# Experts' up projections in steps of 512 inner columns: half-contraction tiles of 512 columns, products of 512, wider evictions and transposes

## The reference, cut to what matters

```python
def swiglu(x, w1, w3, w2):
    return (jax.nn.silu(x @ w1) * (x @ w3)) @ w2
...
    def expert_block(args):
        tok_b, e_b = args
        xb = x2[tok_b]
        return swiglu(xb, w1[e_b], w3[e_b], w2[e_b])
```

## Time and profile before

| what | value |
|---|---|
| median of 3 runs | 3476.21 us (3470.22 to 3481.88) |
| the profiled execution, its own time | 3476.61 us |
| span of its core, first to last instruction | 3474.8 us |
| mean granted TensorE clock over the span | 0.971 |
| PE busy / DVE busy / ACT busy | 3299.8 / 2332.3 / 1838.8 us |
| HBM read | 718.64 MB |

### The profile page before, as it was taken

How to read it: one execution, slowest core, us unless ns; L and a number is a source line. 1 busy time by engine, 2 the same in 40 slices (tenths; PEclk the granted TensorE clock), 3 DMA queues, 4 the chain that set the end, 5 groups by cost and what they waited for, 6 DMA issues and landing times.

```text
span 3474.8 us, 56477 instructions
## 1 busy us (share of the span) xinstructions
PE 3299.8 (95%) x24379; PEld 3047.0 (88%) x24379; DVE 2332.3 (67%) x2986; ACT 1838.8 (53%) x2194; POOL 0.2 (0%) x4
## 2 busy tenths in 40 slices
PE   8999999999899899999999999899799999999798
PEld 7988999999889799999999999888587889985698
DVE  6876655578766588888888888745565556465454
ACT  5464544454635377777777777633443444335343
POOL 0000000000000000000000000000000000000000
PEclk9999999999999899999999999999799999999899
DMA  6432565454325599899899899611233456530353
GB/s 249 170 134 97 182 231 194 158 194 146 134 97 184 214 373 351 327 355 350 333 351 352 334 352 344 252 68 61 109 111 134 141 222 233 211 127 13 134 191 112
DMA packets 102815, 723.43 MB, mean 208 GB/s; under 512 B 11680, under 2 KB 13344, under 8 KB 16672
## 3 DMA queue, kind: packets, MB, share of 16 engines
q1 hardware_dynamic: 102560, 719.73, 56.3%
HBM read 718.64 MB, written 1.05 MB: 207 GB/s over the span
## 4 chain that ended last, share of the span: by engine, by line
PE 77%; DVE 12%; ACT 8%; issue 2%; DMA 1%; SPq 0%; DVEq 0%; ACTq 0%
PE PS L1534 13%; PE PS L1535 13%; PE PS L1536 13%; PE PS L1487 6%; PE PS L1485 6%; PE PS L1486 6%; DVE WL L2244 4%; ACT WH L1855 3%; PE PS L1793 3%; PE PS L1791 3%; PE PS L1792 3%; PE PS L1632 2%; PE PS L1601 2%; PE PS L1564 1%; PE PS L1577 1%
## 5 line engine op out<-in xcount | busy, mean ns | idle before, releaser
L2244 DVE TENSOR_TENSOR WL<-RAW,WH 128x2048 fp32r<-128x2048 f32 (+2 forms) x428 | 963.0, 2252 | 578.0 <-ACT WH L1855 572.4
L1855 ACT ACTIVATE WH<-RAW 128x2048 fp32r<-128x2048 f32 (+2 forms) x428 | 802.6, 1878 | 252.7 <-PE PS L1536 183.6
L1534 PE MATMUL PS<-PH,WH 128*128 128x256 f32 x2464 | 710.8, 288 | 39.2 <-DVE PL L2440 7.9
L1536 PE MATMUL PS<-PH,WL 128*128 128x256 f32 x2464 | 697.2, 283 | 0.0
L1535 PE MATMUL PS<-PL,WH 128*128 128x256 f32 x2464 | 697.2, 283 | 0.0
L2244 DVE TENSOR_TENSOR WL<-F,WH 128x2048 fp32r<-128x2048 f32 x210 | 481.2, 2292 | 87.4 <-ACT WH L1855 86.4
L1534 PE MATMUL PS<-HPH,WH 128*128 128x256 f32 (+1 forms) x1648 | 496.7, 301 | 24.6 <-DVE HPL L2330 12.6
L1534 PEld LDWEIGHTS PS<-PH,WH 128*128 128x128 f32 x2464 | 471.2, 191 | 47.9 <-issue 29.2
L1535 PE MATMUL PS<-HPL,WH 128*128 128x256 f32 (+1 forms) x1648 | 481.2, 292 | 0.0
L1536 PE MATMUL PS<-HPH,WL 128*128 128x256 f32 (+1 forms) x1648 | 480.8, 292 | 0.0
L1535 PEld LDWEIGHTS PS<-PL,WH 128*128 128x128 f32 x2464 | 471.1, 191 | 1.3
(11 more groups left out here) (382 smaller groups left out, 5072.8 us busy)
## 6 DMA issues: line engine op xcount, KB each, us to landing
F<-in_moe_w SPq DMA_DIRECT2D x210, 1024.0 KB, 5.5
RAW<-in_ffn_w SPq DMA_DIRECT2D x130, 1024.0 KB, 4.9
RAW<-in_moe_w SPq DMA_DIRECT2D x126, 1024.0 KB, 5.1
RAW<-in_w_in SPq DMA_DIRECT2D x64, 1024.0 KB, 4.9
F<-in_ada_w SPq DMA_DIRECT2D x18, 1024.0 KB, 11.5
RAW<-in_w_kv SPq DMA_DIRECT2D x16, 1024.0 KB, 4.9
G<-in_ada_w SPq DMA_DIRECT2D x15, 1024.0 KB, 10.4
RAW<-in_w_in_ab SPq DMA_DIRECT2D x12, 1024.0 KB, 5.0
```

Of the source, the lines that this page charges most:

```text
L1534: T_.matmul(out, lh, rh, start=first, stop=False)
L1536: last = T_.matmul(out, ll, rh, start=False, stop=end)
L1855: S.activation(mem["WH"][:, t.s % NHL, 0:m], v.raws[t.slot][:, 0:m], ACT.Copy).then_inc(*ac.done("w_hi", t.s))
L2244: V.tensor_tensor(mem["WL"][:, t.s % NHL, 0:m], v.raws[t.slot][:, 0:m], mem["WH"][:, t.s % NHL, 0:m].bitcast(F32), sub).then_inc(*dv.done( ...
```

## The change

The up tiles are cut the other way: 512 rows of 512 columns in place of 1024 rows of 256. The bytes and the number of tiles stay (1 MB, 28 up tiles and 14 down tiles per expert), and the host lays `moe_w1` and `moe_w3` out for it. A step now covers 512 inner columns, so there are 7 per expert:

- `up(e, j, which, half)` handles one tile: 4 row blocks x 3 = 12 matmuls of 512 columns, into a whole bank; `half` 0 starts the sum and `half` 1 ends it.
- The silu eviction, the gate multiplication, and the two copies after the transposes are 512 columns wide and half as many; `turn` does four transposes.
- The order within a step is up `w1` half 0, turn (step before), up `w1` half 1, up `w3` half 0, down, up `w3` half 1, down. `finish`, `sel`, `gather` and `context_sums` hang on the same positions (`beside`), at twice the pace per step; in the last expert two sums and the norm's middle go behind the last `turn`.
- The silu on ACT now waits for the second `w1` tile in the unit of that tile. `TMP1` is used as two rows of 512 in place of four of 256, and the ring of turned rows holds two double steps.

```diff
-    def up(e, j, which):
-        t = p.weight(("up", part, e, j, which), io["moe_w1" if which == 0 else "moe_w3"][e], j)
-        t.end = ("up", part, e, j, which)
+    def up(e, j, which, half):
+        t = p.weight(("up", part, e, j, which, half), io["moe_w1" if which == 0 else "moe_w3"][e], 7 * half + j, 4, 512)
+        t.end = ("up", part, e, j, which, half)
         out.append(("tile", t.key))
-        p.bank(t.end, MOEB)
-        if which == 1:
-            p.tmp.take(("tmp", "moe", part, e, j), TMP4)
-        put("up", e, j, which)
+        if half == 0:
+            p.bank(("up", part, e, j, which), MOEB)
+        elif which == 0:
+            p.tmp.take(("tmp", "moe", part, e, j), (0, 2))
+        put("up", e, j, which, half)
...
+    def beside(e, j, at):
+        if j == 1 and at == 0 and e:
+            finish(e - 1)
+        if e % 2 and e < 7:
+            if j == 3 and at == 0:
+                put("sel", e + 1)
+            elif j > 3 and 2 * j - 8 + at < 5:
+                gather(e + 1, 2 * j - 8 + at)
+        if e == 7 and part == 0 and 2 * j + at > 6:
+            context_sums(2 * j - 7 + at)
     for e in range(8):
-        for j in range(14):
-            pe_, pj = (e, j - 1) if j else (e - 1, 13)
-            up(e, j, 0)
+        for j in range(7):
+            pe_, pj = (e, j - 1) if j else (e - 1, 6)
+            up(e, j, 0, 0)
             if pe_ >= 0:
                 turn(pe_, pj)
-            up(e, j, 1)
+            up(e, j, 0, 1)
+            up(e, j, 1, 0)
+            if pe_ >= 0 and (e, j) != (7, 6):
+                down(pe_, 2 * pj)
+            beside(e, j, 0)
+            up(e, j, 1, 1)
+            if (e, j) == (7, 6):
+                down(pe_, 2 * pj)
             if pe_ >= 0:
-                down(pe_, pj)
-                if pj == 13:
+                down(pe_, 2 * pj + 1)
+                if pj == 6:
                     put("leave", pe_)
...
+            beside(e, j, 1)
+    turn(7, 6)
+    if part == 0:
+        for k in (7, 8, 9):
+            context_sums(k)
+    down(7, 12)
     down(7, 13)
...
-        out = bank(key)[:, 0:256]
-        product(out, [(v.xg(e, 0, k), v.xg(e, 1, k), w.h[:, k, :], w.l[:, k, :]) for k in range(8)]).then_inc(*pe.done("ps", *key))
+        if half == 0:
+            pe.freed(plan.banks.before[key])
+        out = PS[:, plan.banks.place[key], :]
+        for k in range(4):
+            xh, xl = v.xg(e, 0, 4 * half + k), v.xg(e, 1, 4 * half + k)
+            T_.matmul(out, xh, w.h[:, k, :], start=half == 0 and k == 0, stop=False)
+            T_.matmul(out, xh, w.l[:, k, :], start=False, stop=False)
+            last = T_.matmul(out, xl, w.h[:, k, :], start=False, stop=half == 1 and k == 3)
+        last.then_inc(*pe.done("ps", *key, half))
...
-        for k in range(2):
+        for k in range(4):
             last = T_.transpose(out[:, k * 128:k * 128 + 128], tm[:, k * 128:k * 128 + 128], ident)
...
-        if which:
+        if which == 0 and half == 1:
             key = ("tmp", "moe", part, e_, j)
-            ac.wait_ge("ps", "up", part, e_, j, 0)
+            ac.wait_ge("ps", "up", part, e_, j, 0, 1)
...
-        if which:
-            key = ("tmp", "moe", part, e_, j)
-            y = mem["TMP1"][:, plan.tmp.place[key], :]
+        if which and half:
+            y = v.hid(plan.tmp.place["tmp", "moe", part, e_, j])
```

More of the change, by code:

```diff
@@ L708, in splits_ahead @@
         elif kind == "up":
-            at["up", args[3], args[0], args[1], args[2]] = pos
+            at["up", args[4], args[0], args[1], args[2], args[3]] = pos
         elif kind == "down":
@@ L884, in first_order @@
             p.apply("f1")
-            p.put("tile", ("up", 0, 0, 0, 0), 1)
+            p.put("tile", ("up", 0, 0, 0, 0, 0), 1)
             p.bank(("router",), (7,))
@@ L1390, in views, with hs @@
     v.gate_col = lambda e: mem["GC"][:, e % 3:e % 3 + 1]
-    v.hs = lambda e, j: (p2.h[:, (14 * e + j) % 4, :], p2.l[:, (14 * e + j) % 4, :])
+    def hs(e, j, n=1):
+        i = (14 * e + j) % 4
+        return tuple(x[:, i:i + n, :].rearrange("p a n -> p (a n)") for x in (p2.h, p2.l))
+    v.hs = hs
+    v.hid = lambda i: mem["TMP1"][:, i:i + 2, :].rearrange("p a n -> p (a n)")
     return v
@@ L1763, in gather, with up @@
             last.then_inc(*pe.done("ps", "g", part, e, i))
-    def up(e, j, which, part):
+    def up(e, j, which, half, part):
         key = ("up", part, e, j, which)
-        w = weight(key)
-        for i in range(8):
+        w = weight(key + (half,))
+        for i in (0, 1, 4, 5) if half == 0 else (2, 3, 6, 7):
             pe.wait_ge("free_a", "g", part, e - e % 2, i)
-        out = bank(key)[:, 0:256]
-        product(out, [(v.xg(e, 0, k), v.xg(e, 1, k), w.h[:, k, :], w.l[:, k, :]) for k in range(8)]).then_inc(*pe.done("ps", *key))
+        if half == 0:
[7 more added lines that the diff above has]
+        last.then_inc(*pe.done("ps", *key, half))
     def turn(e, j, part):
-        out, tm = bank(("tr", part, e, j)), mem["TMP1"][:, plan.tmp.place["tmp", "moe", part, e, j], :]
+        out, tm = bank(("tr", part, e, j)), v.hid(plan.tmp.place["tmp", "moe", part, e, j])
         pe.wait_ge("free_d", "up", part, e, j, 1)
-        for k in range(2):
+        for k in range(4):
             last = T_.transpose(out[:, k * 128:k * 128 + 128], tm[:, k * 128:k * 128 + 128], ident)
@@ L1782, in down @@
         w, (oh, ol) = weight(("dn", part, e, j)), v.hs(e, j)
-        pe.wait_ge("free_d", "tr", part, e, j)
+        pe.wait_ge("free_d", "tr", part, e, j // 2)
         if j == 0 and e:
@@ L2114, in gather @@
                 if x >= 3:
-                    ac.wait_ge("ps", "up", part, x - 3, 13, 1)
+                    ac.wait_ge("ps", "up", part, x - 3, 6, 1, 1)
                 dst = v.xg(x, i // 4, 2 * (i % 4), 2).rearrange("p (k c) -> p k c", k=2)
@@ L2118, in gather, with up @@
             last.then_inc(*ac.done("free_a", "g", part, e_, i))
-    def up(e_, j, which, part):
-        if which:
+    def up(e_, j, which, half, part):
+        if which == 0 and half == 1:
             key = ("tmp", "moe", part, e_, j)
-            ac.wait_ge("ps", "up", part, e_, j, 0)
+            ac.wait_ge("ps", "up", part, e_, j, 0, 1)
             ac.freed(plan.tmp.before[key])
-            S.activation(mem["TMP1"][:, plan.tmp.place[key], :], bank(("up", part, e_, j, 0))[:, 0:256], ACT.Silu).then_inc(
+            S.activation(v.hid(plan.tmp.place[key]), bank(("up", part, e_, j, 0)), ACT.Silu).then_inc(
                 *ac.done("free_a", "up", part, e_, j, 0))
@@ L2129, in turn @@
         ac.wait_ge("ps", "tr", part, e_, j)
-        n = 14 * e_ + j
+        n = 14 * e_ + 2 * j
         if n >= 4:
-            ac.wait_ge("ps", "dn", part, (n - 4) // 14, (n - 4) % 14)
-        S.activation(v.hs(e_, j)[0], bank(("tr", part, e_, j))[:, 0:256], ACT.Copy).then_inc(*ac.done("hs_hi", part, e_, j))
+            ac.wait_ge("ps", "dn", part, (n - 3) // 14, (n - 3) % 14)
+        S.activation(v.hs(e_, 2 * j, 2)[0], bank(("tr", part, e_, j)), ACT.Copy).then_inc(*ac.done("hs_hi", part, e_, j))
     def leave(e_, part):
@@ L2694, in gather, with up @@
             V.tensor_copy(v.gate_col(x), bank(("g", part, x, "gc"))[:, 0:1]).then_inc(*dv.done("free_d", "g", part, x, "gc"))
-    def up(e_, j, which, part):
-        if which:
-            key = ("tmp", "moe", part, e_, j)
-            y = mem["TMP1"][:, plan.tmp.place[key], :]
+    def up(e_, j, which, half, part):
+        if which and half:
+            y = v.hid(plan.tmp.place["tmp", "moe", part, e_, j])
             dv.wait_ge("free_d", "g", part, e_, "gc")
             dv.wait_ge("free_a", "up", part, e_, j, 0)
-            dv.wait_ge("ps", "up", part, e_, j, 1)
-            V.scalar_tensor_tensor(y, y, v.gate_col(e_), bank(("up", part, e_, j, 1))[:, 0:256], mult, mult).then_inc(
+            dv.wait_ge("ps", "up", part, e_, j, 1, 1)
+            V.scalar_tensor_tensor(y, y, v.gate_col(e_), bank(("up", part, e_, j, 1)), mult, mult).then_inc(
                 *dv.done("free_d", "up", part, e_, j, 1))
     def turn(e_, j, part):
-        oh, ol = v.hs(e_, j)
+        oh, ol = v.hs(e_, 2 * j, 2)
         dv.wait_ge("hs_hi", part, e_, j)
-        V.tensor_tensor(ol, bank(("tr", part, e_, j))[:, 0:256], oh.bitcast(F32), sub).then_inc(*dv.done("free_d", "tr", part, e_, j))
+        V.tensor_tensor(ol, bank(("tr", part, e_, j)), oh.bitcast(F32), sub).then_inc(*dv.done("free_d", "tr", part, e_, j))
     def leave(e_, part):
@@ L3003, in lay_out @@
         "w_in_ab": packed(x["w_in_ab_2"][0]), "w_out_ab": packed(x["w_out_ab_2"][0]), "w_out_c": packed(x["w_out_c_2"][0], 2, 1024),
-        "moe_w1": np.stack([packed(w) for w in x["moe_w1"][0]]), "moe_w3": np.stack([packed(w) for w in x["moe_w3"][0]]),
+        "moe_w1": np.stack([packed(w, 4, 512) for w in x["moe_w1"][0]]), "moe_w3": np.stack([packed(w, 4, 512) for w in x["moe_w3"][0]]),
         "moe_w2": np.stack([packed(w, 2, 1024) for w in x["moe_w2"][0]]),
```

10 lines of the change are left out of this document (removed).

## The result

| | kernel before | changed kernel |
|---|---|---|
| median, range (5 runs each) | 3471.42 us (3470.16 to 3481.88) | 3451.3 us (3447.54 to 3459.14) |
| ratio, 95% interval | 1 | 0.9936 [0.9916, 0.9956] |
| profiled execution, its span | 3476.61 us, 3474.8 us | 3447.54 us, 3445.8 us |

The change makes the kernel faster by 20 us. Of the 7.7 us between 3459.0 and 3451.3, 3476.2 - 3471.4 = 4.8 come from the level that the sum started from, a median of three runs, and 20.1 - 17.2 = 2.9 from the size of the gain.

A forecast was written before the change was run, and what follows sets the result against it. PE was taken to bound the experts' stretch; 16.7 us from up products plus 0.7 at the end came off 3476.61 us, other terms 0, giving 3459.0 against the median. Range 3451 to 3471, main case 3454 to 3465 (81%).

The forecast's parts named there:

- the spare times: Slack before PE wants a low half in plain double steps: 0.66 us behind the silu, 0.68 us behind the turn.
- The bound, and the up products: Experts' stretch goes at PE's pace; 12 products of 512 columns replace 24 of 256, saving 0.075 us per tile, 16.7 us.
- the `down` row: Profile row of the same step's down tile: 12 products of 512 columns in 2.80 us, taken as the new up price.
- the two rivals that priced the product at 0.240 or half way: Up products: no fixed cost saved, 3475.5 us, chance 8%; or only half the gain, 3467.1 us, chance 7%.
- the forecast's estimate of 0.03 us per tile: Up products by the skill's rule, N/2.4 + 2.5 ns: 2.62 against 2.59 us per tile, 6.7 us in all; not adopted.
- The slower rival: Second `w3` tile's low half comes late every double step once its path is 0.66 us longer; 3494 us, chance 4%.
- Copies, banks, transposes, loads: Wider evictions, bank reuse, four transposes per double step and weight loads: each taken as 0; transposes might save 4.5 us.
- The two ends: Last expert's end: one PE wait instead of two (0.98 + 1.02 us), gain 0.7 us, between -0.6 and 2; start gains nothing.
- The clock: One half-clock dip of about 3.4 us in a gather step, costing 1.7 us, may go, stay or double: 0 +- 2.
- A clock below 1.00 in the stretch: Listed among the signs that would show the forecast wrong: PE's clock falling within the experts' stretch.
- The sum: 16.7 us from up products plus 0.7 from the end: 17.4 us off the profiled 3476.61, giving 3459.0 against the median.
- The low end of the range, 3451: Wide range's lower edge, reached if cheaper transposes (up to 4.5 us) and one clock dip less come together.

## Why the forecast was wrong, and which of its steps held

The pace of the stretch, its bound and the spare times came out as forecast. What was wrong is the step from the stretch to the total, and inside the stretch several terms are off that cancel.

*The bound, and the up products: right, a little small.* The stretch goes at PE's pace, and an up tile took the pace of the `down` row, 2.80 us. The kernel with narrow products shows that this, and no other part, carries the gain. The forecast took 0.075 us a tile from starts given to 0.01 us, between 0.07 and 0.08. The seven double steps say 0.080 each, 17.8 us for 223 tiles in place of 16.7; and by the same rows the two rivals that priced the product at 0.240 or half way fall: they would have given double steps of 17.6 and 17.4. So does the forecast's estimate of 0.03 us per tile, worked out from the rule that the Trainium skill gives for an isolated product (page "TensorE: Matmul & The Clock Gate", section "Back-to-back issue gap"); this trace, with 0.080, does not agree with it.

*The slower rival: false, and its threshold right.* No split came late. The kernels with extra silus put the point from which it decides between 0.52 and 0.92 us of added path; the forecast said 0.66. Past that point a double step with a late split lost 0.43 us.

*Copies, banks, transposes, loads: right.* 599, 741, 683 and 600 ns against estimates of 580, 740, 680 and 600. Four transposes cost what two pairs did. Loads never held anything up: a window of plain double steps (1510 to 1544.5 us) moved 363 GB/s, where the forecast had reckoned with 365, with PE busy throughout. No wait of PE stands at a gather or a `leave` of a plain step. A double step with a `finish` is 19.57 us before and 19.14 after, so it lost 0.11 us more than a plain one; seven of them are 0.8 us that the forecast had no term for.

*The two ends: gain about twice as large.* At the end PE idles 0.56 us where the kernel before idled 0.98 + 1.02: 1.4 us in place of 0.7, since the norm sums stand inside the wait. At the start the two waits of 1.02 us of the kernel before (the second is the `WL` wait of the earlier trace rows) became one of 2.16.

*The clock: past its bound.* Three dips of about 3.4 us at half the clock (1.2 GHz) lie in the changed kernel's stretch, near 1210, 1660 and 1914 us, where before had one. "A clock below 1.00 in the stretch" was one of the forecast's own signs of being wrong, and it came. A double step of the second gather with a dip is 22.15 us, the one of the first gather without one 20.61 (turn to turn), so a dip costs 1.5 us here, and in the kernel before 21.38 - 19.99 = 1.4; the difference of the two kernels is 3 x 1.5 - 1.4 = 3.1 us, where the forecast allowed 2. Ahead of the second and the third PE was busy without a pause, at a granted clock of 1.00 (1640 to 1659 us, 1895 to 1912 us). What stands just ahead of both is the first step of a gather, some 2.2 us of products of 8 rows and of one column, as it does ahead of the dip of the earlier trace rows:

```profile
1657.27 0.60 PE L1774 MATMUL PS<-SM,PH 128*128 128x1 f32 x4
...
1659.68 0.57 PE L1796 MATMUL PS<-WH,PH 128*128 128x512 f32 x1
```

Not every such step is followed by a dip: in the nine profiles in which it is not cut in two, 13 of 27 are.

*The sum.* In the stretch 17.8 + 1.4 + 0.8 - 3.1 = 16.9 us by these terms, 17.2 measured. The kernel with narrow products fits them: without the 17.8 it should keep 1.4 + 0.8, less 1.6 for one dip more than before, 0.6 us, and it kept 1.1. So the 17.4 of the forecast came out near the measured 17.2 by luck: up products, ends and `finish` gave 2.6 us more than the sum had, and the dips took 3.1 back.

*What failed* is the step from the stretch to the total. The sum was set against one execution "0.4 us above the median shown", as if three runs fixed the level at 3476.2; the kernel before measured 3471.4, 3472.1, 3475.0 and 3475.3 later on. And the sum has no term for what lies behind the stretch: it puts that at nothing without a reason, while the same 8272 matmuls took 1228.3 to 1242.3 us there in ten profiles. The changed kernel measured 21 us less in all and 17 in the stretch: 4 us that no term has. The low end of the range, 3451, was to be reached by transposes that cost less and a dip that goes; four transposes cost 0.46 us, as two pairs did, and two dips came on top. That 3451.3 lies beside that end is luck.

*What stays open.* Whether these 4 us are real. 17.2 us would be a ratio of 0.9950, which lies inside each of the three intervals. On the other hand, in all eight measurements of wide tiles (narrow products among them) the median fell by more than the stretch did, by 0.6 to 8.6 us, and in that of the old tiles in another order by 0.6 less; several of them share their runs of the kernel before, so they are fewer than eight witnesses.

Behind the stretch the two profiles of old tiles show 1242.3 and 1240.8 us, the eight of wide tiles 1228.3 to 1239.1, with a mean of 1234.8. That hints at some microseconds gained there, though no instruction there was changed, and with two profiles of one kind it proves nothing. The granted clock of that part is 0.95 or 0.96 in every profile, and PE's busy time moves along with its length (1144.1 in the shortest, 1156.7 in one of the longest), so the half-clock spells in it are the likeliest carrier. An estimate from windows of 1 us, PE's busy time in each times what the granted clock lacked of 1.00, puts what they cost there at 40.8 us in the shortest profile, 49.8 in both of the old tiles and 54.4 in the third longest; it explains part of the scatter and not all. Why they would fall better behind wide tiles was not tested, nor was the layout of `moe_w1` and `moe_w3` in memory, which differs too.

## What to carry to other kernels

Where matmuls set the pace, take the price of another width from a row of the same stage with the same operands' buffers, by starts and not by busy time, and over a whole tile rather than one product; then count how late the widened evictions make the next stage's input, because that spare (here 0.67 us in 17.25) decides between a gain and a loss. Set the range from the scatter of the parts the change doesn't touch: compare at least two profiles cut at the same instructions before a difference of spans is put down to the change.

## What the runs showed of the hardware that was not expected

- Products of 256 columns cost 0.120 us each in `up` (2.88 us for 24) and 0.117 in an earlier stage; at 512 columns that excess is gone (0.2333 for each, in `up` as in `down`). Neither the order of the three products nor the wide tile's layout changes it. Its cause is open.
- The clock dips sit at nearly the same place in repeated profiles of one kernel (near 1210, 1660 and 1914 us in two of the three, 1211, 1409 and 1914 in the third), those past the first tiles each within 3 us of the start of a gather's first step, and move when a wait is taken away: without the 2.16 us wait at the first tiles the dip beside it was gone.
- Work on an engine with spare time is not quite free: an extra 0.52 us on ACT per double step, which made nothing late, still cost 1.9 us over the stretch, in stalls of PE's weight loads with no releaser in the profile.
